# Gate and up projections of a decoder block as a 2x2 block product with seven half products

## What is computed

```python
u = _rmsnorm(x, g_mix)
z = u @ w_in + b_in                       # q | k | v | x branch | y branch
attn = windowed attention with sinks; lru = RG-LRU of a causal convolution
mix = jnp.concatenate([attn, lru * jax.nn.gelu(yb)], axis=-1)
h = x + mix @ w_out + b_out
gate, up = jnp.split(_rmsnorm(h, g_ffn) @ w_ffn_in, [D_FF], axis=-1)
y = h + (jax.nn.silu(gate) * up) @ w_ffn_out
```

## Time and profile before

| | |
|---|---|
| median of three runs | 2334.68 us (2333.93 to 2334.83) |
| span of the profiled execution | 2331.0 us |
| TensorE busy | 97% of the span |
| VectorE, ScalarE, GpSimd busy | 56%, 38%, 1% |
| matmuls | 12165 |
| moved by DMA | 207.34 MB, mean 89 GB/s |

### The profile page before, as it was taken

How to read it: one execution, slowest core, us unless ns; L and a number is a source line. 1 busy time by engine, 2 the same in 40 slices (tenths; PEclk the granted TensorE clock), 3 DMA queues, 4 the chain that set the end, 5 groups by cost and what they waited for, 6 DMA issues and landing times.

```text
span 2331.0 us, 31209 instructions
## 1 busy us (share of the span) xinstructions
PE 2251.5 (97%) x12165; PEld 1915.8 (82%) x12165; DVE 1302.4 (56%) x2146; ACT 878.1 (38%) x1349; POOL 32.4 (1%) x66
## 2 busy tenths in 40 slices
PE   6999999999999999999999999999999899999996
PEld 6777888888777888888877788888888799999996
DVE  4786535356587544445668653545668665444453
ACT  4574223235375322223457432323446532222221
POOL 1000000000000000000000000000000000000000
PEclk9999999999999999999999999999999899999998
DMA  4123232323313233332322323233231122222221
GB/s 148 55 68 114 91 100 90 101 89 92 101 46 118 91 97 93 92 98 92 107 67 63 119 91 98 91 97 94 92 124 45 30 91 86 87 91 82 92 80 60
DMA packets 58586, 207.34 MB, mean 89 GB/s; under 512 B 7341, under 2 KB 7549, under 8 KB 58416
## 3 DMA queue, kind: packets, MB, share of 16 engines
q1 hardware_dynamic: 51840, 184.57, 25.5%
q0 software_dynamic: 3936, 12.03, 1.5%
q10 hardware_dynamic: 2656, 8.62, 1.0%
HBM read 196.44 MB, written 9.77 MB: 88 GB/s over the span
## 4 chain that ended last, share of the span: by engine, by line
PE 84%; DVE 9%; ACT 4%; issue 2%; DMA 1%; ACTq 0%; DVEq 0%; POOL 0%
PE bank L533 27%; PE bank L535 27%; PE bank L534 27%; DVE s_p L1258 2%; DVE w_lo L1157 1%; DVE xc L1297 1%; PE bank L661 1%; ACT s_p L961 1%; DVE om L1326 1%; PE bank L628 1%; DVE pT L1277 1%; PE bank L583 1%; ACT L986 0%; PE bank L557 0%; DVE ii L1325 0%
## 5 line engine op out<-in xcount | busy, mean ns | idle before, releaser
L533 PE MATMUL bank<-x_hi,w_hi 128*128 128x512 f32 (+1 forms) x2320 | 826.4, 356 | 3.7 <-DVE x_lo L1187 2.6
L535 PE MATMUL bank<-x_hi,w_lo 128*128 128x512 f32 (+1 forms) x2320 | 820.3, 354 | 0.0
L534 PE MATMUL bank<-x_lo,w_hi 128*128 128x512 f32 (+1 forms) x2320 | 819.5, 353 | 0.0
L883 ACT ACTIVATE w_hi<-w_raw 128x1024 fp32r<-128x1024 f32 (+1 forms) x360 | 374.1, 1040 | 1175.3 <-PE bank L535 1175.3
L533 PEld LDWEIGHTS bank<-x_hi,w_hi 128*128 128x128 f32 x2320 | 438.9, 189 | 79.8 <-issue 13.6
L1157 DVE TENSOR_TENSOR w_lo<-w_raw,w_hi 128x1024 fp32r<-128x1024 f32 (+1 forms) x360 | 431.8, 1200 | 127.7 <-ACT w_hi L883 125.9
L534 PEld LDWEIGHTS bank<-x_lo,w_hi 128*128 128x128 f32 x2320 | 439.1, 189 | 61.8 <-issue 1.4
L535 PEld LDWEIGHTS bank<-x_hi,w_lo 128*128 128x128 f32 x2320 | 438.3, 189 | 60.8
L533 PE MATMUL bank<-a_hi,w_hi 128*128 128x512 f32 (+1 forms) x1200 | 427.4, 356 | 6.2 <-DVE a_lo L1561 1.8
L535 PE MATMUL bank<-a_hi,w_lo 128*128 128x512 f32 (+1 forms) x1200 | 425.0, 354 | 0.0
L534 PE MATMUL bank<-a_lo,w_hi 128*128 128x512 f32 (+1 forms) x1200 | 424.3, 354 | 0.0
(11 more groups left out here) (240 smaller groups left out, 1475.0 us busy)
## 6 DMA issues: line engine op xcount, KB each, us to landing
w_raw<-in_units SPq DMA_DIRECT2D x296, 512.0 KB, 3.5
w_raw<-in_units SPq DMA_DIRECT2D x64, 448.0 KB, 3.3
x_tok<-in_x_prompt POOLq DMA_DIRECT2D x16, 512.0 KB, 6.1
out_y_p<-y_tok ACTq DMA_DIRECT2D x16, 512.0 KB, 3.0
gfin<-in_g_fin POOLq DMA_DIRECT2D x1, 512.0 KB, 7.1
kc_tok<-in_cache_k POOLq DMA_DIRECT2D x1, 512.0 KB, 6.9
vc_tok<-in_cache_v POOLq DMA_DIRECT2D x1, 512.0 KB, 7.3
out_nk_s<-in_cache_k POOLq DMA_DIRECT2D x1, 496.0 KB, 6.5
```

The lines of the kernel that those rows point to most:

```text
L533: nc.tensor.matmul(out, h, hi[:, kt, c0:c1], start=(first and kt == kts[0]), stop=False)
L534: nc.tensor.matmul(out, h, lo[:, kt, c0:c1], start=False, stop=False)
L535: mm = nc.tensor.matmul(out, l, hi[:, kt, c0:c1], start=False, stop=(kt == kt_of[u] - 1))
L883: w_hi_ready.by(A(w_hi[:, u % RING, 0:n], w_raw[:, u % RAW, 0:n], ACT.Copy))
```

## The change

Gate tile and up tile of one hidden tile are taken as one group g. Its weights are a 2x2 block matrix: B11 and B21 are the first and second half (4 k tiles each) of the gate unit, B12 and B22 those of the up unit. The normed activations are a 2x2 block matrix too: two halves of the tokens by two halves of the features. In place of eight half products there are seven, on sums of blocks:

- weight sums, on GpSimd (`weight_sums`): T1 = B12 - B11 and T3 = B22 - B12 in one instruction of 2 x 512 columns, then T2 = T1 - B22 and T4 = T2 + B21 of 512 columns each. Those of group g+1 are made while group g runs, those of a chunk's first group behind the last chunk.
- activation sums, once a block in `h_tile`: seven blocks `xo_hi`, `xo_lo` (A11, A12, A22 and S1 to S4) of 256 or 272 columns, made of tiles m and m+4. The output tiles therefore go in the order `M_ORDER` = 0, 4, 1, 5, 2, 6, 3, 7.
- products p1 to p7 (`product`), each 4 k tiles x 3 matmuls of 256 (narrow) or 272 (wide) columns, into banks a, bb, cc of one of two sets. TensorE's order is p1, p2, p4 of the group before, p6, p5, p7, p3. p6 and p7 go on adding into p1's bank and p3 into p5's, so ScalarE copies out what stood there first (`keep`, `keep_c21`).
- VectorE adds the kept parts and the banks to the four blocks of gate and up (`c11`, `c22`, `c12`), and multiplies gate and up by `rinv` in two operations of their own on SBUF tiles (`gate`, first line of `hidden`). The rest of the hidden tile's steps stays.
- splits go by pieces: b1 (B11 and B21, 1024 columns), t21 (T2 and T1, 1024), t3, b22 and t4 (512 each), in a ring of six halves (`HALVES`).
- raw weights have four places, two of them (`w_raw2`) over the recurrent branch's buffers, so the first group's load waits for the last `lmix_ready`.
- chunks are 6, 8 and 8 hidden tiles, and the down stage of each begins with most k tiles of two units.
- the x loads are issued from ScalarE's queue after the last group, because their buffer now lies over `xo`; the x tiles of the next block follow down units 2 to 7 (`X_AT`). The samples' input projection moves from block 0's to the last block's head, and the loop is Fori(0, NB - 2) with the third block written out behind it.

The parts of the diff that matter:

```diff
-    FCH = []
+    HCH = []
     n = -(-NF // KT)
     for i in range(n):
-        FCH.append(NF // n + (i < NF % n))
+        HCH.append(NF // n + (i < NF % n))
+    FCH = []
+    left = NF
+    while left:
+        FCH.insert(0, min(KT, left))
+        left -= FCH[0]
...
+    PIECES = [("u", u) for u in range(UD0)]
+    for ci, nf in enumerate(FCH):
+        for g in range(F0[ci], F0[ci] + nf):
+            PIECES.append(("b1", g))
+            if g > F0[ci]:
+                PIECES.append(("t4", g - 1))
+            PIECES += [("t21", g), ("t3", g), ("b22", g)]
+        PIECES.append(("t4", F0[ci] + nf - 1))
+        PIECES += [("u", u) for u in U_OUT[ci]]
...
+            def weight_sums(b, g):
+                n = load_of["g", g, 0]
+                raw_landed(pool, b, n)
+                raw_landed(pool, b, n + 1)
+                if g == 0:
+                    freed.wait(pool, b, UO0 + 4)
+                else:
+                    w_ready.wait(pool, b, piece_of["t3", g - 1] + 1)
...
+                both = w_raw if raw_at[n] < 2 else w_raw2
+                t13_done.by(TT(t_w[:, T1:T3 + 1:T3 - T1, 0:KH * P],
+                               both[:, 1, :].rearrange("p (o q) -> p o q", o=2), both[:, 0:2, 0:KH * P], ALU.subtract))
+                t13_done.wait(pool, b, g + 1)
+                t2_done.by(TT(t_w[:, T2, 0:KH * P], t_w[:, T1, 0:KH * P], both[:, 1, KH * P:], ALU.subtract))
+                t2_done.wait(pool, b, g + 1)
+                w_ready.wait(pool, b, max(piece_of["b1", g], piece_of.get(("t4", g - 1), 0)) + 1)
+                t4_done.by(TT(t_w[:, T4, 0:KH * P], t_w[:, T2, 0:KH * P], both[:, 0, KH * P:], ALU.add))
...
+            def product(b, last, g, name, out, xo, start=False, kts=range(KH)):
+                key, half = {"p1": ("b1", 0), "p2": ("b1", 1), "p6": ("t21", 0), "p5": ("t21", 1), "p7": ("t3", 0),
+                             "p3": ("b22", 0), "p4": ("t4", 0)}[name]
+                w = H if last else T // 2
+                w_ready.wait(pe, b, piece_of[key, g] + 1)
+                at = (half_of[key, g] + half) % HALVES * KH * P
+                for kt in kts:
+                    if g == 0:
+                        xo_ready.wait(pe, b, 4 * kt + {A11: 1, S3: 2, A12: 3, A22: 3}.get(xo, 4))
+                    h = w_hi[:, at + kt * P:at + (kt + 1) * P]
+                    l = w_lo[:, at + kt * P:at + (kt + 1) * P]
+                    x_h, x_l = xo_hi[:, xo, kt, 0:w], xo_lo[:, xo, kt, 0:w]
+                    nc.tensor.matmul(out[:, 0:w], h, x_h, start=(start and kt == 0), stop=False, skip_group_check=True)
+                    nc.tensor.matmul(out[:, 0:w], h, x_l, start=False, stop=False, skip_group_check=True)
+                    mm = nc.tensor.matmul(out[:, 0:w], l, x_h, start=False, stop=(kt == KH - 1), skip_group_check=True)
+                if kts[-1] == KH - 1:
+                    prod_done.by(mm)
...
+                a, bb, cc = SUMS[g % 2]
...
+                product(b, last, g, "p1", a, A11, True)
+                if g > 1:
+                    c11_ready.wait(pe, b, g - 1)
+                if g == 0:
+                    early, late = range(KH - 1), [KH - 1]
+                    product(b, last, g, "p2", cc, A12, True, early)
+                    p1_kept.wait(pe, b, g + 1)
+                    product(b, last, g, "p6", a, S2, False, early)
+                    product(b, last, g, "p5", bb, S1, True, early)
+                    product(b, last, g, "p2", cc, A12, True, late)
+                    product(b, last, g, "p6", a, S2, False, late)
+                    sqh_added.wait(pe, b, KT)
+                    amix_ready.wait(pe, b, QB)
+                    stath_done.by(feature_sums(last))
+                    product(b, last, g, "p5", bb, S1, True, late)
+                else:
+                    product(b, last, g, "p2", cc, A12, True)
+                    if g > F0[ci]:
+                        finish(b, last, g - 1)
+                    p1_kept.wait(pe, b, g + 1)
+                    product(b, last, g, "p6", a, S2)
+                    if g > 1:
+                        c12_ready.wait(pe, b, g - 1)
+                    product(b, last, g, "p5", bb, S1, True)
+                u2_kept.wait(pe, b, g + 1)
+                product(b, last, g, "p7", a, S3)
+                p5_kept.wait(pe, b, g + 1)
+                product(b, last, g, "p3", bb, S4)
+            def finish(b, last, g):
+                c22_ready.wait(pe, b, g + 1)
+                product(b, last, g, "p4", SUMS[g % 2][0], A22)
...
+                    most, end_ = list(range(nf - 1)), [nf - 1]
+                    lead = [(0, 0), (0, 1)] if last else [(0, 0), (1, 0)]
+                    for m, c in lead:
+                        gemm(b, last, U_OUT[ci][m], a_hi, a_lo, act_tile, most, c)
+                    for m, c in lead:
+                        gemm(b, last, U_OUT[ci][m], a_hi, a_lo, act_tile, end_, c)
...
+                def keep(g, name, dst, read, kept):
+                    prod_done.wait(act, b, prod_of[name, g])
+                    read.wait(act, b, g)
+                    src = SUMS[g % 2][1 if name == "p5" else 0][:, 0:h]
+                    kept.by(A(dst, src, ACT.Copy))
+                def keep_c21(g):
+                    prod_done.wait(act, b, prod_of["p4", g])
+                    c21_kept.by(A(gt[:, g % 2, h:w], SUMS[g % 2][0][:, 0:h], ACT.Copy))
...
+                        split(b, ("t3", g))
+                        keep(g, "p1", p1s, c11_ready, p1_kept)
+                        split(b, ("b22", g))
+                        if f > 0:
+                            keep_c21(g - 1)
+                        if f < nf - 1:
+                            split(b, ("b1", g + 1))
+                        keep(g, "p6", u2s, c12_ready, u2_kept)
+                        if g == 0:
                             stath_done.wait(act, b, 1)
                             rms(last, stdh_ready)
...
+                        split(b, ("t4", g))
+                        if f > 0:
+                            gate(g - 1)
+                        keep(g, "p5", p5s, c22_ready, p5_kept)
+                        if f < nf - 1:
+                            split(b, ("t21", g + 1))
+                        else:
+                            split(b, ("u", U_OUT[ci][0]))
+                        if f > 0:
+                            hidden_hi(g - 1, f - 1)
...
+                h, k = w // 2, m % KH
+                add_square(b, wide, M_ORDER.index(m), ssum, sq[:, 0], sqh_ready, sqh_added)
...
+                g1 = v(VG2 + k)
+                s1, s2, s4 = (x_s_[:, i, 0:h] for i in range(3))
+                ins = TS(x_g[:, 0:w], hT[:, m, 0:w], v(VG2 + m), None, ALU.mult)
+                xs_ready.by(ins)
+                xs_ready.wait(dve, b, 3 * k + 2)
+                link(STT(out=s1, in0=hT[:, k, h:w], scalar=g1, in1=x_g[:, h:w], op0=ALU.mult, op1=ALU.add))
+                link(STT(out=s2, in0=hT[:, k, 0:h], scalar=g1, in1=s1, op0=ALU.mult, op1=ALU.subtract))
+                xs_ready.by(TT(s4, x_g[:, 0:h], s2, ALU.add))
+                xo_hi_ready.wait(dve, b, n + 3)
+                xo_ready.by(TT(xo_lo[:, A12:A22 + 1, k, 0:h], x_g[:, 0:w].rearrange("p (o q) -> p o q", o=2),
+                               xo_hi[:, A12:A22 + 1, k, 0:h], ALU.subtract))
+                xs_ready.wait(dve, b, 3 * k + 3)
+                xo_hi_ready.wait(dve, b, n + 4)
+                xo_ready.by(TT(xo_lo[:, S1:S4 + 1, k, 0:h], x_s_[:, :, 0:h], xo_hi[:, S1:S4 + 1, k, 0:h],
+                               ALU.subtract))
...
+                def add(g, name, n, dst, kept_as, kept, ready):
+                    prod_done.wait(dve, b, prod_of[name, g])
+                    kept.wait(dve, b, g + 1)
+                    ready.by(TT(dst, SUMS[g % 2][n][:, 0:h], kept_as, ALU.add))
+                def c11(g):
+                    if g == 0:
+                        xo_ready.wait(dve, b, 4 * KH)
+                    add(g, "p2", 2, gt[:, g % 2, 0:h], p1s, p1_kept, c11_ready)
+                def c22(g):
+                    add(g, "p7", 0, t_w[:, up_at[g % 2], h:w], p5s, p5_kept, c22_ready)
+                def c12(g):
+                    add(g, "p3", 1, t_w[:, up_at[g % 2], 0:h], u2s, u2_kept, c12_ready)
+                def gate(g):
+                    c21_kept.wait(dve, b, g + 1)
+                    c11_ready.wait(dve, b, g + 1)
+                    gate_ready.by(TT(gt[:, g % 2, 0:w], gt[:, g % 2, 0:w], rinv[:, 0:w], ALU.mult))
+                def hidden(g):
+                    u = t_w[:, up_at[g % 2], 0:w]
+                    c12_ready.wait(dve, b, g + 1)
+                    up_ready.by(TT(u, u, rinv[:, 0:w], ALU.mult))
+                    gate_tanh.wait(dve, b, g + 1)
+                    link(STT(out=gt[:, g % 2, 0:w], in0=th[:, 0:w], scalar=1.0, in1=gt[:, g % 2, 0:w],
+                             op0=ALU.add, op1=ALU.mult))
+                    up_ready.wait(dve, b, g + 1)
```

(68 more changed lines are left out.)

621 lines of the change are left out of this document (407 added, 214 removed).

## The result

| | before | after |
|---|---|---|
| median | 2334.3 us | 2369.9 us (2367.0 to 2374.1) |
| ratio | | 1.0156 [1.0141, 1.0170] |
| span of the profiled execution | 2331.0 us | 2365.0 us |
| narrow block, from one FFN norm sum to the next (mean of two) | 554.2 us | 563.6 us |
| from the last FFN norm sum to the end | 424.7 us | 410.5 us |

The account below looks back on a forecast made before the run. TensorE was taken to bound the kernel. From the 2331.0 us span: -111.1 for fewer matmuls, +8.8 ScalarE, +4 edges, -1 start, giving 2231.7, plus 3.7 to the median: 2235 us (-4.3%), chance 0.43; range 2219 to 2415.

Parts of the forecast that it names:

- What bounds the kernel now: Gate, up and down stage: TensorE busy from end to end at full clock, so a matmul removed is time removed.
- 2.2 for ScalarE: ScalarE's copies out of banks delay TensorE by 0.1 us a group, between 0 and 0.4; 8.8 us over 88 groups.
- 1.1 at the edge: Group 0 of a block: the last k tile's combinations leave 1.1 us exposed a block, +4 us in all.
- Narrow and wide group: 84 matmuls a group: narrow 9.97 us for 11.15, wide 10.57 for 12.08; together 111.1 us saved.
- The line between the two forms: 256-column matmul time taken from a line through the 512- and 272-column times: 0.1187 us each.
- rival 3: Floor: a 256-column matmul costs the 272-column time, +40 us, 2275 us; chance 0.04.
- VectorE's own 8.3 us: VectorE's work in a narrow group sums to 8.3 us against TensorE's 9.97, leaving 1.7 us to spare.
- GpSimd's 4.0 us: GpSimd's weight sums, 2048 columns a group, priced as two memset streams: 4.0 us, between 2.0 and 6.0, covered.
- By that I take no slowdown: VectorE beside GpSimd's sums: no slowdown, since VectorE's multiply kept 0.69 us beside GpSimd's issue of x loads.
- Rival 1: Exclusion: VectorE and GpSimd wait for each other when both read two SBUF tiles; 12.4 us a group, 2376 us; chance 0.42.
- Start: Samples' load no longer precedes block 0, but the token load must land anyway; only its transposes go, -1 us.
- rival 2: Lateness: sums, t21's split and ScalarE's copies come 0.3 to 1.2 us a group late, 2260 to 2340; chance 0.11.

Follow-up runs that it names:

- e1: Changed kernel with GpSimd's three weight sums replaced by memsets of the same columns, each behind an 8-column sum that takes the waits; 2239.2 us, 0.961 of before.
- e4: Changed kernel with all three weight sums made on VectorE, none on GpSimd; 2283.6 us, 0.980 of before.
- e2: Changed kernel with GpSimd's sums replaced by copies that read one tile, each behind an 8-column sum; 2241.7 us, 0.962 of before.
- e10: Changed kernel with splits from the third group on taking one operand from a bank and the gate's scale a one-input multiply; 2265.6 us, 0.972 of before.

## Why the prediction was wrong, step by step

- **What bounds the kernel now**: right. TensorE did, and the seven products were worth what was said: in e1 a narrow block takes 530.6 us for 554.2 before, 23.6 less, where the sum had 22.7 (22 x 1.18, less 2.2 for ScalarE and 1.1 at the edge).
- **Narrow and wide group**: right. e1, which takes away GpSimd's reading and shortens its work, has 10.00 us a group for 9.97, and 2239.2 us in all for the 2235 of the sum. The line between the two forms of the earlier trace rows held for 256 columns, so rival 3 (2275) is out. In the wide block a group takes 10.59 us in e1 (gate scales at 2091.19 and 2101.78) for 10.57.
- **VectorE's own 8.3 us**: right, by e4: 10.87 less the three sums from start to start (1.25 + 0.61 + 0.61) and a gap of 0.1 is 8.3. Its 1.7 us of margin is what e2 lives on.
- **GpSimd's 4.0 us**: too low; measured a quarter more. Without contention the sums take 2.39 + 1.28 + 1.28 = 4.95 us, 2.3 to 2.5 ns a column, so neither two streams (1.9) nor three (2.85) of the memset of the earlier trace rows. The Trainium skill's figure (GPSIMD Engine Reference, Elementwise — side-by-side cycle accounting), 4497 ns for 2048 columns, is 2.2 ns a column and would have been the better price.
- **"By that I take no slowdown"**: this is the step that failed. The earlier trace rows show GpSimd issuing transfers beside VectorE, no tile being read, and the text said so, yet took it as the nearest row. What the runs showed in its place: a steady group's VectorE work of 8.3 us is stretched by some 4 us, to 12.27, and VectorE becomes the bound over TensorE's 9.97. There was no row in the trace of before that could speak on it: GpSimd computed nothing after its memsets there. With no row, the chances of forecast and rival were close (0.43 and 0.42), and the order between them rested on a row that didn't bear on the question.
- **Rival 1** gave the mechanism and nearly the size: a group of 12.4 us (12.27 measured), +141 (130.7 between e1 and the changed kernel), 2376 (2369.9). Part of that closeness is luck: its sums were 0.95 us too cheap, and of the real sums' 4.95 us only 4.05 reach VectorE as stretch, so the two cancel. Against e1, exclusion costs 33 us a narrow block (563.6 for 530.6) and 23 at the wide end (410.5 for 387.6); the rival's sum had 37 and 31. And it was stated too narrowly, for both engines reading two tiles; e2 shows that one is enough on GpSimd's side, e10 that it can be enough on VectorE's.
- **Start**: predicted -1, measured +6.7 at the first norm sum (32.4 to 39.0) of the profiled run. The move of the x load was costed for later blocks and not for block 0, where GpSimd's queue loses its first item. That the loads queued behind it would then run beside it wasn't considered.
- **ScalarE and rival 2**: no lateness of its own. The sign that the prediction had named for it, TensorE idle until ScalarE's copy, did appear, 58.5 us, but behind a held VectorE; it falls to 9.2 us in e1, which ends 4 us above the sum, and part of that is its start.

The range, 2219 to 2415, held the time because it took in the rival.
